# A hybrid decoder step: rounded key-value and mid-state products, and the samples' state updates moved into the output projection

## The reference

```python
def retention_chunk(q, k, v, s_prev, log_gamma):
    ...
    scores = jnp.einsum('bhnd,bhmd->bhnm', q, k) * decay_mask[None].astype(q.dtype)
    inner = jnp.einsum('bhnm,bhme->bhne', scores, v)
    cross_decay = jnp.exp(log_gamma[:, None] * (n[None, :] + 1.0))
    cross = jnp.einsum('bhnd,bhde->bhne', q, s_prev.astype(q.dtype)) * cross_decay[None, :, :, None].astype(q.dtype)
    k_decay = jnp.exp(log_gamma[:, None] * (L - 1.0 - n[None, :]))
    kv = jnp.einsum('bhmd,bhme->bhde', k * k_decay[None, :, :, None].astype(k.dtype), v)
    s_new = jnp.exp(log_gamma * L)[None, :, None, None] * s_prev + kv
    return inner + cross, s_new.astype(s_prev.dtype)
```

## Time and profile before

| | |
|---|---|
| median of 3 runs | 1459.53 us (1459.17 to 1459.82) |
| the profiled execution | 1459.5 us, its span 1457.7 us |
| TensorE busy | 1451.0 us |
| VectorE, ScalarE busy | 798.6, 543.5 us |
| retention with its four heads | to 494 us of the span |
| DMA | 171.9 MB, mean 118 GB/s |

### The profile page before, as it was taken

How to read it: one execution, slowest core, us unless ns; L and a number is a source line. 1 busy time by engine, 2 the same in 40 slices (tenths; PEclk the granted TensorE clock), 3 DMA queues, 4 the chain that set the end, 5 groups by cost and what they waited for, 6 DMA issues and landing times.

```text
span 1457.7 us, 27410 instructions
## 1 busy us (share of the span) xinstructions
PE 1451.0 (100%) x11460; PEld 1396.8 (96%) x11460; DVE 798.6 (55%) x1063; ACT 543.5 (37%) x776; POOL 3.4 (0%) x25
## 2 busy tenths in 40 slices
PE   9999999999999999999999999999999999999998
PEld 8699789879969999999999999999999999999998
DVE  7785577468458855555552327444565555553222
ACT  5552273264155633333331324222343333332222
POOL 0000000000000000000000000000000000000000
PEclk9999999999999999999999999999999999999999
DMA  8445253463444322222222222223222222223221
GB/s 300 147 187 183 102 214 118 170 228 108 177 155 184 102 93 96 86 86 96 91 90 88 100 88 87 87 89 101 89 87 98 89 86 95 92 86 99 94 87 59
DMA packets 47743, 171.91 MB, mean 118 GB/s; under 512 B 5608, under 2 KB 6248, under 8 KB 46624
## 3 DMA queue, kind: packets, MB, share of 16 engines
q1 hardware_dynamic: 47488, 170.71, 33.7%
q0 software_dynamic: 32, 0.03, 0.0%
q10 hardware_dynamic: 144, 0.00, 0.0%
HBM read 149.39 MB, written 21.55 MB: 117 GB/s over the span
## 4 chain that ended last, share of the span: by engine, by line
issue 100%; POOL 0%; POOLq 0%
POOLq L106 0%; POOL v_tail_stack L281 0%; POOL ident L266 0%; POOL k_tail_stack L275 0%; POOL h_tail L263 0%; POOL mean_v L259 0%; POOL ident L257 0%; POOL h_lo L262 0%; POOL h_hi L261 0%; POOL sample_ones L274 0%; POOL mean_d L258 0%; POOL scores_end_stack L277 0%; POOL late_q_decayed L276 0%; POOL sample_ones L279 0%; POOL seed L268 0%
## 5 line engine op out<-in xcount | busy, mean ns | idle before, releaser
L851 ACT ACTIVATE w_hi<-w_raw 128x1024 fp32r<-128x1024 f32 x227 | 240.0, 1059 | 669.1 <-PE ps L406 469.9
L406 PE MATMUL ps<-h_hi,w_hi 128*128 128x264 f32 (+2 forms) x2300 | 468.3, 285 | 1.5 <-DVE h_lo L1190 1.5
L406 PE MATMUL ps<-h_lo,w_hi 128*128 128x264 f32 (+2 forms) x2300 | 465.3, 284 | 0.0
L406 PE MATMUL ps<-h_hi,w_lo 128*128 128x264 f32 (+2 forms) x2300 | 465.0, 283 | 0.0
L1162 DVE TENSOR_TENSOR w_lo<-w_raw,w_hi 128x1024 fp32r<-128x1024 f32 x227 | 277.1, 1223 | 332.1 <-ACT w_hi L851 331.8
L406 PEld LDWEIGHTS ps<-h_hi,w_hi 128*128 128x128 f32 x2300 | 355.8, 188 | 2.8 <-issue 2.1
L406 PEld LDWEIGHTS ps<-h_hi,w_lo 128*128 128x128 f32 x2300 | 355.5, 188 | 0.0
L406 PEld LDWEIGHTS ps<-h_lo,w_hi 128*128 128x128 f32 x2300 | 355.2, 188 | 0.0
L700 PE MATMUL ps<-z_hi,w_hi 128*128 128x264 f32 (+1 forms) x704 | 144.6, 283 | 0.0
L700 PE MATMUL ps<-z_hi,w_lo 128*128 128x264 f32 (+1 forms) x704 | 144.6, 283 | 0.0
L700 PE MATMUL ps<-z_lo,w_hi 128*128 128x264 f32 (+1 forms) x704 | 144.5, 283 | 0.0
(11 more groups left out here) (208 smaller groups left out, 1413.7 us busy)
## 6 DMA issues: line engine op xcount, KB each, us to landing
w_raw<-in_w_units_dram SPq DMA_DIRECT2D x227, 512.0 KB, 3.2
states<-in_state_ret_dram SPq DMA_DIRECT2D x32, 512.0 KB, 9.0
out_ret_s_dram<-states SPq DMA_DIRECT2D x32, 512.0 KB, 4.7
v_bcast<-v_scratch SPq DMA_DIRECT2D x8, 1024.0 KB, 5.7
x_res<-in_x_all_dram SPq DMA_DIRECT2D x8, 268.0 KB, 6.1
out_ret_p_dram<-tmp SPq DMA_DIRECT2D x4, 512.0 KB, 3.8
out_y_prompt_dram<-y_rows SPq DMA_DIRECT2D x4, 512.0 KB, 2.6
decay<-in_decay_dram SPq DMA_DIRECT2D x4, 287.0 KB, 3.9
```

The lines of the kernel that those rows point to most:

```text
L406: out = mm(PS[:, 2 * s + half, at:at + n_col], a, b[:, lo:lo + n_col], start=first and n == 0, stop=last and n == 2)
L851: fn(WH[:, c % NS, :], RAW[:, c % NR, :], ACT.Copy).then_inc(hi_ready, 1)
```

## The change

Three things. (1) Keys, values, mid state and decayed late queries get hi and lo parts, and their products are made of three rounded ones; for that ScalarE and VectorE write the parts, ScalarE now reads all four blocks of values (twice each), and the sum of the two halves of the state takes two additions. (2) The samples' rows no longer have a product of their own: their hi and lo rows stand in free rows of the stacked tail operand (24 and up of each 32), which now has 128 rows, and `v_tail_stack` is first written whole. (3) Outer products and updates move into the output projection, by a table that says which samples follow which pair p, for the last head up into the first FFN units; the spread values are loaded later, the next head's first four states are loaded ahead of unit 4, and loads of the next units now stand between the stores.

The core of the diff:

```diff
+UPDATES = (((), (0, 1), (2, 3), (4, 5, 6, 7)), ((0, 1), (2, 3), (), ()))
...
@@ SyncE
+            def head(h, first, last):
...
+                if not first:
+                    for b in range(4):
+                        load_state(b)
+                for n in range(4, 6):
                     in_heads(h, n)
...
-                for b in range(NB):
-                    if not first:
-                        sp.wait_ge(s_out[b], 16 * h)
-                    sp.dma_start(S[:, b, :], st_in[b, h]).then_inc(s_in[b], 16)
+                for b in range(0 if first else 4, NB):
+                    load_state(b)
...
-                for b in range(NB):
-                    sp.wait_ge(s_upd, NB * h + (b + 1))
-                    sp.dma_start(st_out[b, h], S[:, b, :]).then_inc(s_out[b], 16)
...
                 for n in range(14, 16):
                     in_heads(h, n)
+                for n in range(2):
+                    next_unit(h, n)
+                for p in range(4):
+                    for b in UPDATES[last][p]:
+                        store_state(h, b)
+                    if p in (1, 2):
+                        next_unit(h, 1 + p)
+                if last:
+                    ffn_in_unit(0, 1, 0)
+                    for b in range(4, NB):
+                        store_state(h, b)
@@ TensorE
-                pe.wait_ge(kn_ready, 4 * h + 4)
                 for js in ((0, 1), (2, 3, 4)):
                     for e in range(2):
                         if js[0] == 2:
-                            pe.wait_ge(mid_ready, 2 * h + e + 1)
+                            pe.wait_ge(mid_lo, 2 * h + e + 1)
+                        else:
+                            pe.wait_ge(kn_lo, 4 * h + 2 * e + 2)
+                            pe.wait_ge(v_lo, 4 * h + 4)
                         for j in js[:2]:
-                            out = mm(PS[:, 6 + e, :], KN[:, j, e * P:(e + 1) * P], V[:, j, :], start=j in (0, 2), stop=j == 1)
+                            kh, kl = KNH[:, j, e * P:(e + 1) * P], KNL[:, j, e * P:(e + 1) * P]
+                            for q, (k, v) in enumerate(((kh, VH), (kh, VL), (kl, VH))):
+                                out = mm(PS[:, 6 + e, :], k, v[:, j, :], start=j in (0, 2) and q == 0, stop=j == 1 and q == 2)
...
                     for e in range(2):
-                        mm(PS[:, 2 * s + 1, 0:N_LATE + NB], KM[:, e * DV + dt * P:e * DV + (dt + 1) * P], QL[:, e, :], start=e == 0, stop=False)
+                        km = slice(e * DV + dt * P, e * DV + (dt + 1) * P)
+                        for q, (k, c) in enumerate(((KMH, QLH), (KMH, QLL), (KML, QLH))):
+                            mm(PS[:, 2 * s + 1, 0:N_LATE + NB], k[:, km], c[:, e, :], start=e == 0 and q == 0, stop=False)
...
-                    mm(PS[:, 2 * s + 1, 4 * P - CUT:T - CUT], VS[0:96, vt], SS[0:96, :], start=False, stop=False)
-                    out = mm(PS[:, 2 * s + 1, TP - CUT:T - CUT], OS[:, vt], SEL[:], start=False, stop=True)
+                    out = mm(PS[:, 2 * s + 1, 4 * P - CUT:T - CUT], VS[:, vt], SS[:], start=False, stop=True)
@@ ScalarE
-                for b in (0, 2):
-                    act.wait_ge(v_acc, 3 * h + b + 1)
+                for b in range(4):
+                    if b < 3:
+                        act.wait_ge(v_acc, 3 * h + b + 1)
+                    else:
+                        act.wait_ge(unit_done, U_HEAD * h + (NS + 8))
                     fn(V[:, b, :], PS[:, 2 + b, :], ACT.Copy, scale=RN[:, b:b + 1]).then_inc(v_ready, 1)
+                    fn(VH[:, b, :], PS[:, 2 + b, :], ACT.Copy, scale=RN[:, b:b + 1]).then_inc(v_hi, 1)
...
                 for p in range(4):
                     if not (last and p == 3):
                         split_hi(12 + p + NS, U_HEAD, h)
+                    for b in UPDATES[last][p]:
+                        outer(h, b)
@@ ScalarE, FFN
+                    if first and l == 0:
+                        for b in range(4, NB):
+                            outer(HEADS - 1, b)
@@ VectorE
-                tt(KV, PS[:, 6:8, :].rearrange("p e v -> p (e v)"), KM, ALU.add).then_inc(kv_ready, 1)
+                tt(KV, PS[:, 6:8, :].rearrange("p e v -> p (e v)"), KMH[:].bitcast(F32), ALU.add).then_inc(kv_sum, 1)
+                dve.wait_ge(kv_sum, h + 1)
+                tt(KV, KV, KML[:].bitcast(F32), ALU.add).then_inc(kv_ready, 1)
...
                         for k in (2 * p, 2 * p + 1):
                             norm_tile(k, 1, C_RET, N_RET, D_FFN)
+                    for b in UPDATES[last][p]:
+                        update(h, b)
@@ VectorE, FFN
+                        if l == 0:
+                            for b in range(4, NB):
+                                update(HEADS - 1, b)
```

More of the change, by code:

```diff
@@ L115, in build @@
         WL = sb("w_lo", [P, NS, UNIT], F32R)
+        with ExitStack() as s8:
+            KMH = sb("mid_state_hi", [P, 2 * DV], F32R, scope=s8)
+            KML = sb("mid_state_lo", [P, 2 * DV], F32R, scope=s8)
         TMP = sb("tmp", [P, 5, T])
@@ L326, in _, with ffn_in_unit, next_unit, store_state @@
             sp.dma_start(CF[:], io["ffn_consts"]).then_inc(ffn_in, 16)
-            def head(h, first):
-                for n in range(4 if first else 0, 6):
+            def ffn_in_unit(l, i, n):
+                load(U_FFN_IN[l] + 4 * i + n)
+            def next_unit(h, n):
+                if h < HEADS - 1:
+                    in_heads(h + 1, n)
+                else:
+                    ffn_in_unit(0, 0, n)
+            def store_state(h, b):
+                sp.wait_ge(s_upd, NB * h + (b + 1))
+                sp.dma_start(st_out[b, h], S[:, b, :]).then_inc(s_out[b], 16)
+            def head(h, first, last):
+                def load_state(b):
+                    if not first:
+                        sp.wait_ge(s_out[b], 16 * h)
+                    sp.dma_start(S[:, b, :], st_in[b, h]).then_inc(s_in[b], 16)
+                if not first:
+                    for b in range(4):
+                        load_state(b)
+                for n in range(4, 6):
                     in_heads(h, n)
@@ L352, in head @@
                 sp.dma_start(kv_dst[h], KV).then_inc(kv_sent, 16)
-                for b in range(NB):
-                    sp.wait_ge(s_upd, NB * h + (b + 1))
-                    sp.dma_start(st_out[b, h], S[:, b, :]).then_inc(s_out[b], 16)
+                sp.wait_ge(v_sent, 16 * h + 16)
+                sp.wait_ge(inner_done, 4 * h + 4)
+                for half in range(2):
+                    b = half * NB // 2
+                    sp.dma_start(VB[:, b:b + NB // 2, :], VSCR[b:b + NB // 2, :].partition_broadcast(P)).then_inc(vb_in[half], 16)
                 for n in range(14, 16):
                     in_heads(h, n)
+                for n in range(2):
[9 more added lines that the diff above has]
+                        store_state(h, b)
             for h in range(HEADS):
-                head(h, h == 0)
+                head(h, h == 0, h == HEADS - 1)
             for l in range(2):
@@ L366, in ffn_units @@
             def ffn_units(l):
-                with sp.Fori(0, JF // 2) as i:
+                if l == 1:
+                    for n in range(4):
+                        ffn_in_unit(l, 0, n)
+                for n in range(1 if l == 0 else 0, 4):
+                    ffn_in_unit(l, 1, n)
+                with sp.Fori(2, JF // 2) as i:
                     for n in range(4):
@@ L913, in _, with outer @@
             fn(RN[:], PS[:, 3, 300:305], ACT.Sqrt, bias=EPST[:]).then_inc(rows_rstd, 2)
+            def outer(h, b):
+                if b == 0:
+                    act.wait_ge(z_mul, 8 * h + 8)
+                if b in (0, NB // 2):
+                    act.wait_ge(vb_in[b // (NB // 2)], 16 * h + 16)
+                if b >= 2:
+                    act.wait_ge(s_upd, 8 * h + (b - 1))
+                for e in range(2):
+                    at = (b % 2) * 1024 + e * DV
+                    fn(G[:, at:at + DV], VB[:, b, :], ACT.Copy, scale=KD8[:, e, b:b + 1]).then_inc(samp_kv, 1)
             def head(h, first, last):
@@ L1027, in _ @@
                 head(h, h == 0, h == HEADS - 1)
-            for b in range(NB):
-                act.wait_ge(s_out[b], 16 * HEADS)
             def ffn(l, norm_no):
@@ L1054, in body @@
                     split_hi(u0 + 3 + NS, 4, i)
+                    if first and l == 0:
+                        for b in range(NB):
+                            act.wait_ge(s_out[b], 16 * HEADS)
                     for t in range(2):
@@ L1672, in shape_constants @@
         decay[h, 0:16, DEC_TAIL:DEC_TAIL + 16] = decay[h, 0:16, 0:16]
-        decay[h, 16:24, DEC_TAIL + 16:] = np.eye(NB)
+        decay[h, 16:24, DEC_TAIL + 16:DEC_TAIL + 24] = np.eye(NB)
+        for b in range(NB):
+            row = TILE * (b % 4) + 24 + b - b % 4
+            decay[h, row:row + 2, DEC_STACK + 16 + b] = 1.0
+            decay[h, row + 1, DEC_MASK] = -1.0
```

169 lines of the change are left out of this document (85 added, 84 removed).

## The result

The changed kernel takes 1497.7 us (median of 4 runs, 1495.0 to 1499.1), beside 1459.55 us of the kernel before on the same chip: a ratio of 1.026, 95% interval [1.0248, 1.0272], 38 us slower. The forecast was 1489.1 us, slower, in a range of 1468 to 1504 us: the sign and the range hold. The sum is 8.6 us short, and the measured time lies 1.7 us above the narrower 1480 to 1496 us to which the forecast gave 0.57. The profiled execution, the slowest of the four (1499.1 us), has a span of 1497.3 us.

A forecast was written before the change was run, and what follows sets the result against it. The prediction took TensorE's stream plus whatever makes TensorE wait as the bound. 1459.5 - 7.3 (stream) + 23.4 (boundaries) + 10.5 (last head) + 3 (clock) = 1489.1 us, range 1468 to 1504, narrower 1480 to 1496 at 0.57.

The forecast's parts named there:

- the stream: TensorE in four heads: rounded products save 3.0 us a head, less a 1.2 us wait for mid_state_lo; -7.3 us in all.
- the boundaries: Three boundaries between heads: TensorE waits for rotations held up by late units 20 and 21, 7.8 us each, +23.4 us.
- the last head: Output projection and first FFN part: TensorE waits 5.7 us for x tiles and 4.8 us for the sum of squares.
- the term for the clock: At the three boundaries between heads: 1 us each for the clock, +3 us in all.
- a granted clock below full after the waits: Listed sign that the forecast is wrong: TensorE's granted clock is below full after its waits; no size given.
- the cases that got 0.12: Whole kernel: a lower clock, or nothing saved by the split; together chance 0.12.
- wait for `mid_state_lo`: Before the second half of each head's key-value products: TensorE waits 1.2 us for VectorE's low part of the mid state.
- the split saves nothing: Rival: six rounded products cost as much as two fp32 ones, waits as forecast, 1501 us; shares 0.12 with lower clock.
- half hidden: Rival: loads don't queue behind states, or the update chain is 3 to 4 us shorter; 1471 us, chance 0.20.
- Faster: Rival: updates are hidden if SyncE's loads come early enough; 1452 us, or 1447 without the mid_state_lo wait; chance 0.08.

The follow-up runs named there:

- e5: Changed kernel, with VectorE writing each half of mid_state_lo ahead of the decayed queries of the same half: 1492.3 us.
- e4: Changed kernel, with 32 more products that nothing reads on TensorE ahead of the values' products of heads 1 to 3: 1493.3 us.
- e1: Changed kernel, with SyncE's loads of units 20 and 21 ahead of the next head's first four state loads: 1480.65 us.
- e2: As e1, and units 18 and 19 (in the last head units 2 and 3 of the FFN) loaded ahead of all stores: 1458.34 us.
- e6: As e2, with all eight updates of the last head in the first FFN part, their stores behind that part's unit loads: 1453.8 us.
- e7: e6 and e5 together, on the changed kernel: 1450.5 us.
- e3: Changed kernel, with all loads and stores of the states issued by GpSimd instead of SyncE: 1461.3 us.

## Why the prediction was right, and what it missed

The forecast was right in kind in its terms for the stream, the boundaries and the last head, and these hold in size too. It was wrong in size in the term for the clock: among its signs of being wrong it lists "a granted clock below full after the waits", and that is what came. The measured 1497.7 us lies above the 1480 to 1496 us drawn round its sum; the range held because it had been drawn up to 1504 us for the cases that got 0.12. Term by term:

| term | forecast | measured | from |
|---|---|---|---|
| shorter stream less the late state, 4 heads | -7.3 | -6.6 | stages |
| of it: wait for `mid_state_lo`, a head | 1.2 | 0.94 | waits, `e5` |
| three boundaries | +23.4 | +25.0 | stages |
| last head without the clock | +10.5 | +9.4 (in part an estimate) | stages, clock |
| lower clock | +3 | +11.1 (3.1 of it an estimate) | stages, `e4` |

- *Stream.* The key-value products with their wait are 0.07 us shorter, where 0.2 was forecast; without the wait 0.99 (`e5`), where 1.4 was. The output products give 1.58 where 1.6 was forecast. The six rounded products with the mid state stand as far apart as the step took, and the samples' row product is gone. Timeline of TensorE, last head:

```profile
463.89 0.38 PE L649 MATMUL ps<-late_q_hi,mid_state_hi 128*128 128x280 f32 x1
464.10 0.29 PE L649 MATMUL ps<-late_q_lo,mid_state_hi 128*128 128x280 f32 x1
464.23 0.29 PE L649 MATMUL ps<-late_q_hi,mid_state_lo 128*128 128x280 f32 x1
```

  0.13 us from start to start, 0.129 forecast (0.21 at the first of the six, so the group takes 0.86 us, not 0.77). The rival that the split saves nothing falls.
- *Boundaries.* The chain of the forecast (store, load, round, rest, update, with the states ahead of units 20 and 21) is what the trace shows, and `e1` and `e2` show it by taking it away in two parts, 15 us and the last 9.5. The first one waited 9.70 us where 8.4 were worked out: on the forecast's time axis (1.8 us later) its units 20 and 21 are issued at 149.8, as worked out, but land at 158.3 and 159.6, 1.1 us later. The others waited 7.3 and 7.5; I took 7.8. At the second one unit 19 took 4.0 us from issue to rounding, at the first 5.5. The waits are 24.5 us where 23.4 were taken, so the mean is better than the parts. The rival "half hidden" falls, since loads do queue behind the states.
- *Faster.* This rival named the thing that decides: with SyncE's loads early enough the updates in heads 0 to 2 are hidden (`e2`). It named 1452 us with the last head hidden as well (`e6`: 1453.8), and 1447 without the wait for `mid_state_lo` (`e7`: 1450.5).
- *Last head.* The waits for the x tiles are 3.2 us in two parts and not 5.7 in one: 1.85 at the banks of the pair p = 1, which the step did not foresee, and 1.32 at those of p = 2. Counted from the start of the output projection, VectorE was through with the x tiles of p = 2 after 26.9 us, where 29.0 were worked out. ScalarE rounded the unit with which this chain begins 1.7 us sooner than in the kernel before, where it waited for that unit's load. Timeline of ScalarE in the kernel before:

```profile
481.66 1.06 ACT L851 ACTIVATE w_hi<-w_raw 128x1024 fp32r<-128x1024 f32 x1 [3.98 <-DMA w_raw<-in_w_units_dram]
```

  In the changed kernel it begins at 506.34, 8.9 us after the start of the stage, before 10.6. The sum of squares came 4.5 us late, 4.8 forecast. The first FFN part also waits 1.0 us for `h_lo` of a tile of x, which the step left out. Without the clock the two stages are 9.4 us longer: 12.5, less half of the 6.2 us that TensorE worked at the lower clock (0.50) from 537.6 to 543.8, which is an estimate.
- *Clock.* The term that was mis-sized: "I take 1 us for each of the three boundaries, near the row", and nothing for the last head. It is off by 8.1 us, of the 10.0 us between the sum (1489.1) and the profiled execution (1499.1; the median is 1.4 us lower). No run shows a price of 1 us: in the changed kernel the stages behind the boundaries took 2.66, 2.71 and 2.60 us more at a granted clock that was 0.50 for part of them, and in `e4`, where it stayed at 1.00, 0.09 and 0.10. The row was taken behind the last product of the kernel and showed a clock of 1.00 some 2 us into an idle time; the waits at the boundaries are 3.6 to 4.9 times as long. Nor did the clock stay full behind the last product in every run: at the end of `e1` and of `e3` it fell (to 0.50) 2.4 and 2.5 us after the start of the last product. The granted clock went from 1.00 to 0.50 during each wait (at 158.1 in the first one, 5.4 us after the last key product had started, in the others 3.1) and came back at 168.3, after 5.6 us of products at the lower clock. Each boundary paid 2.6 to 2.7 us and the last head some 3.1. The four executions of the changed kernel order by their mean clock: 0.987 in the two slowest (1499.1 and 1498.45 us), 0.989 in the next (1497.0) and 0.990 in the fastest (1495.0), so part of their scatter goes with this term.

In this trace the granted clock was at 0.50 in four stretches, one at each of the four long waits (9.70, 7.27, 7.53 and 4.47 us): 158.1 to 168.3, 287.8 to 298.0, 417.5 to 427.7 and 536.9 to 543.8 us.

## What to carry to other kernels

Where one engine issues all transfers in program order, moving compute later moves its stores ahead of loads that something waits for; put the loads whose readers stand nearest first, and the stores behind them: here that order alone was worth 39 us, more than the 12 us by which the rounded products were to shorten the stream. When the list of waits names a compute engine, follow its own idle time back until an engine is really working, or a queue. And give a wait of several microseconds on TensorE a price for the clock besides its length: here waits of 7.3 to 9.7 us cost 2.6 to 2.7 us more, and one of 4.5 us some 3.1 (an estimate).

## What was not expected of the hardware

- Short waits went with the lower clock too, and of waits of the same length some did and some didn't. In `e1` the granted clock was at 0.50 for 3.4, 6.8 and 3.4 us around the ends of waits of 2.92, 3.15 and 3.40 us (from 0.5 us after the end of the first, and from 1.0 and 0.5 us before the ends of the others). The same wait of 1.85 us for the x tiles of the last head was followed by 3.4 us at 0.50 in the profiled executions of `e1`, `e3` and `e5`, and by none in those of the changed kernel, `e2` and `e4`. Of the waits behind the extra products of `e4`, 3.06 and 0.73 us were followed by none and 2.27 us by 3.4. What decides it these runs don't show.
- At the first boundary of the changed kernel, with the DMA engines at 388 to 414 GB/s from 150 to 162 us, transfers of 512 KB on SyncE's queue landed in the order of their issue: the first four states from 150.6 to 155.2, units 20 and 21 at 156.51 and 157.78, 1.27 us apart, which is 413 GB/s, and the other four states from 159.7 to 163.4. The place in the queue was the price: with the four states ahead units 20 and 21 took 8.9 us to landing in the median, and 4.9 in `e1`.
- Two later stretches of the FFN work are 0.25 and 0.18 us longer in the changed kernel, and as much in `e6` and `e7` (751.5 to 879.1 us and 1019.4 to 1065.8 in the kernel before). Their products are the same in number, and none stands out as late; the cause is open.
